# The last branch products and their merge in halves (block 1), and the dilated branch one unit earlier (block 2)

## What is computed

```
y = gates[:, :, 0] * (branches[0] @ w_branch[0])
for n in range(1, N_BRANCH):                       # N_BRANCH = 4
    y = y + gates[:, :, n] * (branches[n] @ w_branch[n])
return y @ w_out
```

```
merged = g_a * (y_a @ br_nsa) + g_b * (y_b @ br_dil) + g_c * (y_c @ br_fox)
return merged @ w_out
```

## Time and profile before

| | |
|---|---|
| time, median of 3 runs | 2589.56 us (2586.72 to 2591.66) |
| profiled execution | 2586.87 us, of which span 2585.1 us |
| granted TensorE clock, mean | 0.982 |
| PE busy | 2467.6 us (95%) |
| DVE busy | 1642.1 us (64%) |
| ACT busy | 1202.5 us (47%) |
| POOL busy | 214.4 us (8%) |

### The profile page before, as it was taken

One profiled execution on the slowest core, in us unless ns is written; L12 is line 12 of the kernel. 1 busy time (PEld: TensorE's weight loads), 2 busy tenths in 40 slices (PEclk: granted clock), 3 DMA queues, 4 the chain that ended last, 5 costly groups with the idle time before them and its releaser, 6 DMA issues.

```text
span 2585.1 us, 34304 instructions
## 1 busy us (share of the span) xinstructions
PE 2467.6 (95%) x14089; PEld 2107.8 (82%) x14089; DVE 1642.1 (64%) x2149; ACT 1202.5 (47%) x1441; POOL 214.4 (8%) x334
## 2 busy tenths in 40 slices
PE   7999998999999999899999999989999999998998
PEld 5888997788788899788778888877877879897786
DVE  4775777676776686767677565565455456556544
ACT  4435464433433546344443346934444443693443
POOL 2000002000100000300010000210000000021000
PEclk9999999999999999899999999999999999999999
DMA  8784455786786454678588554445646545444553
GB/s 288 258 287 152 148 168 181 253 290 232 262 285 227 141 151 161 203 261 283 192 276 297 199 149 138 131 157 191 207 154 215 185 157 158 136 134 163 196 185 107
DMA packets 369163, 514.27 MB, mean 199 GB/s; under 512 B 21600, under 2 KB 310614, under 8 KB 369008
## 3 DMA queue, kind: packets, MB, share of 16 engines
q1 hardware_dynamic: 342608, 415.80, 49.8%
q0 software_dynamic: 26400, 96.28, 10.5%
HBM read 510.89 MB, written 1.13 MB: 198 GB/s over the span
## 4 chain that ended last, share of the span: by engine, by line
PE 86%; DVE 6%; ACT 3%; issue 3%; DMA 0%; POOL 0%; SPq 0%; DVEq 0%; POOLq 0%; ACTq 0%
PE ps L1647 79%; DVE lo L1081 2%; PE ps L1693 2%; ACT hi L708 2%; PE ps L1795 1%; PE ps L1669 1%; PE ps L1823 1%; PE ps L1833 1%; PE ps L1842 1%; DVE arena L1140 1%; DMA raw<-in_ffn_w_gu 0%; DVE X L1114 0%; POOL arena L482 0%; DVE arena L1104 0%; ACT arena L748 0%
## 5 line engine op out<-in xcount | busy, mean ns | idle before, releaser
L1081 DVE TENSOR_TENSOR lo<-raw,hi 128x2048 fp32r<-128x2048 f32 (+1 forms) x400 | 916.4, 2292 | 593.1 <-ACT hi L708 592.3
L708 ACT ACTIVATE hi<-raw 128x2048 fp32r<-128x2048 f32 (+1 forms) x400 | 758.0, 1897 | 559.6 <-PE ps L1647 543.6
L1647 PE MATMUL ps<-hi,NH 128*128 128x512 f32 (+3 forms) x1760 | 683.6, 388 | 53.0 <-DVE NL L1569 28.1
L1647 PE MATMUL ps<-hi,NL 128*128 128x512 f32 (+3 forms) x1760 | 674.0, 383 | 0.0
L1647 PE MATMUL ps<-lo,NH 128*128 128x512 f32 (+3 forms) x1760 | 673.5, 383 | 0.0
L1647 PEld LDWEIGHTS ps<-hi,NH 128*128 128x128 f32 x1760 | 338.4, 192 | 127.2 <-DVE lo L1081 30.6
L1647 PE MATMUL ps<-NH,hi 128*128 128x256 f32 x1376 | 394.2, 286 | 0.0
L1647 PEld LDWEIGHTS ps<-hi,NL 128*128 128x128 f32 x1760 | 337.2, 192 | 67.6
L1647 PEld LDWEIGHTS ps<-lo,NH 128*128 128x128 f32 x1760 | 338.0, 192 | 65.0
L1647 PE MATMUL ps<-NL,hi 128*128 128x256 f32 x1376 | 388.0, 282 | 0.0
L1647 PE MATMUL ps<-NH,lo 128*128 128x256 f32 x1376 | 386.7, 281 | 0.0
(11 more groups left out here) (297 smaller groups left out, 2038.4 us busy)
## 6 DMA issues: line engine op xcount, KB each, us to landing
raw<-in_ffn_w_gu SPq DMA_DIRECT2D x176, 512.0 KB, 4.9
raw<-in_ffn_w_in SPq DMA_DIRECT2D x176, 512.0 KB, 4.7
arena<-in_ada_w POOLq DMA_DIRECT2D x72, 1024.0 KB, 7.1
raw<-in_w_in SPq DMA_DIRECT2D x96, 512.0 KB, 4.5
raw<-in_ffn_w_down SPq DMA_DIRECT2D x88, 512.0 KB, 4.7
raw<-in_ffn_w_out SPq DMA_DIRECT2D x88, 512.0 KB, 4.1
raw<-in_mix_w_in SPq DMA_DIRECT2D x86, 512.0 KB, 4.6
raw<-in_w_branch SPq DMA_DIRECT2D x16, 512.0 KB, 3.7
```

The source lines that it names most:

```text
L708: last = nc.scalar.activation(dst, src, ACT.Copy)
L1081: last = nc.vector.tensor_tensor(dst, src, part.bitcast(F32), ALU.subtract)
L1647: last = nc.tensor.matmul(dst, a, b, start=start and k == 0, stop=stop and k == 2, skip_group_check=skip)
```

## The change

Block 1: branches 2 and 3 are no longer multiplied one after the other. When units 27 and 28 are both there, TensorE takes pairs 0 and 1 of branch 2, pairs 0 and 1 of branch 3, then pairs 2 and 3 of branch 2 and of branch 3. Block 2: the dilated branch (n = 2) moves from unit 28 to unit 27, and the fox branch (n = 1) ends the stage alone: unit 27 holds its first chunk beside the dilated weight, unit 28 its other two. In both blocks VectorE and ScalarE merge pairs 0 and 1 ahead of the splits of unit 30, and pairs 2 and 3 behind them. VectorE's `yl` of a half stand after both `y` of that half.

```diff
                     elif u == BR2 + 1:
-                        pieces = rows(i["br_w_fox_2"][l], 0)
+                        pieces = [(lambda s: raw[:, s, 0:1024], i["br_w_fox_2"][l, 0:128, :]),
+                                  (lambda s: raw[:, s, 1024:2048], i["br_w_dil_2"][l])]
                     elif u == BR2 + 2:
-                        pieces = [(lambda s: raw[:, s, 0:1024], i["br_w_fox_2"][l, 256:384, :]),
-                                  (lambda s: raw[:, s, 1024:2048], i["br_w_dil_2"][l])]
+                        pieces = rows(i["br_w_fox_2"][l], 1)
...
-                    if s.block == 2 and u == BR2 + 2:
+                    if s.block == 2 and u == BR2 + 1:
                         for b in range(4):
                             pair = slice(2 * b, 2 * b + 2)
-                            pool.wait_ge(dve_done, at("dve", "gated 1" if b == 3 else f"gated 1 {b}"))
-                            nc.gpsimd.tensor_tensor(T8[:, pair, :], G2[:, pair, :], G2[:, 16 + 2 * b:18 + 2 * b, :],
+                            pool.wait_ge(dve_done, at("dve", "gated 2" if b == 3 else f"gated 2 {b}"))
+                            nc.gpsimd.tensor_tensor(T8[:, pair, :], G2[:, pair, :], G2[:, 8 + 2 * b:10 + 2 * b, :],
...
                     if u:
+                        if u == OUT1 - 1:
+                            gated_parts(range(0, 2))
                         split_hi(s, u + 2)
...
-                gated_parts()
+                gated_parts(range(2, 4))
...
+            def merged(gates, n, sum_before, pairs):
+
+                for b in pairs:
+                    gated(gates, n, (b,))
+                    mine(f"gated {n}" if b == 3 else f"gated {n} {b}")
+                    dve.wait_ge(pool_done, at("pool", f"{sum_before} {b}"))
+                    y = T8[:, 2 * b:2 * b + 2, :]
+                    nc.vector.tensor_tensor(y, y, gates[:, 2 * b:2 * b + 2, :], ALU.add).then_inc(dve_done, done("dve", f"y {b}"))
+                for b in pairs:
                     dve.wait_ge(act_done, at("act", f"yh {b}"))
                     nc.vector.tensor_tensor(NL[:, 2 * b:2 * b + 2, :], T8[:, 2 * b:2 * b + 2, :], NH[:, 2 * b:2 * b + 2, :].bitcast(F32),
                                             ALU.subtract).then_inc(dve_done, done("dve", f"yl {b}"))
...
                 for u in range(OUT1):
-                    if s.block == 2 and u == BR2 + 2:
-                        gated(G2[:, 16:24, :], 1, False, None)
+                    if u == OUT1 - 1:
+                        if s.block == 1:
+                            gated(G[:, 16:24, :], 2, range(0, 2))
+                            merged(G[:, 24:32, :], 3, "sum 2", range(0, 2))
+                            gated(G[:, 16:24, :], 2, range(2, 4))
+                        else:
+                            merged(G2[:, 16:24, :], 1, "sum 1", range(0, 2))
                     if u:
                         split_lo(s, u + 2)
...
+                    if u == OUT1 - 1:
+                        if s.block == 1:
+                            merged(G[:, 24:32, :], 3, "sum 2", range(2, 4))
+                        else:
+                            merged(G2[:, 16:24, :], 1, "sum 1", range(2, 4))
...
+                    if k < 2:
+                        branch_unit(s, k, [(0, 2 * k), (1024, 2 * k + 1)], True, True).then_inc(unit_used, 1)
+                    elif k == 3:
+
+                        ahead = (u - 1) % RING
+                        branch_unit(ahead, 2, [(0, 4), (1024, 5)], True, True, range(0, 2))
+                        branch_unit(s, 3, [(0, 6), (1024, 7)], True, True, range(0, 2))
+                        branch_unit(ahead, 2, [(0, 4), (1024, 5)], True, True, range(2, 4)).then_inc(unit_used, 1)
+                        branch_unit(s, 3, [(0, 6), (1024, 7)], True, True, range(2, 4)).then_inc(unit_used, 1)
...
                 elif u == BR2 + 1:
 
                     pe.wait_ge(act_done, at("act", f"ev {BR2 - 1}"))
-                    last = branch_unit(s, 1, [(0, 3), (1024, 4)], True, False)
+                    branch_unit(s, 1, [(0, 3)], True, False)
+                    last = branch_unit(s, 2, [(1024, 2)], True, True)
                 else:
-                    branch_unit(s, 1, [(0, 5)], False, True)
-                    last = branch_unit(s, 2, [(1024, 2)], True, True)
+                    last = branch_unit(s, 1, [(0, 4), (1024, 5)], False, True)
...
                 out_part(o, 0)
-                if s.block == 2:
+                if s.block == 1:
                     pe.wait_ge(dve_done, at("dve", "gated 2 2"))
                 out_part(o, 1).then_inc(unit_used, 1)
```

More of the change, by code:

```diff
@@ L642, in mix @@
                                                     ALU.add).then_inc(pool_done, done("pool", f"sum {k} {b}"))
-                    if s.block == 2 and u == BR2 + 2:
+                    if s.block == 2 and u == BR2 + 1:
                         for b in range(4):
                             pair = slice(2 * b, 2 * b + 2)
-                            pool.wait_ge(dve_done, at("dve", "gated 1" if b == 3 else f"gated 1 {b}"))
-                            nc.gpsimd.tensor_tensor(T8[:, pair, :], G2[:, pair, :], G2[:, 16 + 2 * b:18 + 2 * b, :],
+                            pool.wait_ge(dve_done, at("dve", "gated 2" if b == 3 else f"gated 2 {b}"))
+                            nc.gpsimd.tensor_tensor(T8[:, pair, :], G2[:, pair, :], G2[:, 8 + 2 * b:10 + 2 * b, :],
                                                     ALU.add).then_inc(pool_done, done("pool", f"sum 1 {b}"))
-                    if u == BR1 + (1 if s.block == 1 else 3):
+                    if u == BR1 + (1 if s.block == 1 else 2):
                         pool.wait_ge(pool_done, at("pool", "sum 1 3"))
@@ L1014, in exps, with gated_parts @@
                             nc.scalar.activation(DE[:, 0, :], DE[:, 0, :], ACT.Exp).then_inc(act_done, done("act", "dexp"))
-            def gated_parts():
-                for b in range(4):
+            def gated_parts(pairs):
+                for b in pairs:
                     act.wait_ge(dve_done, at("dve", f"y {b}"))
@@ L1563, in factors, with gated @@
                                 .then_inc(dve_done, done("dve", f"factor {n}"))
-            def gated(gates, n, last, sum_before):
-                def rest(b):
+            def gated(gates, n, pairs=range(4)):
+                for b in pairs:
+                    dve.wait_ge(pe_done, at("pe", f"br {n} {b}"))
+                    v = gates[:, 2 * b:2 * b + 2, :].rearrange("p a t -> p (a t)")
+                    nc.vector.tensor_tensor(v, v, ps[:, 4 * (1 - n % 2) + b, :], ALU.mult).then_inc(dve_done, done("dve", f"gated {n}" if b == 3 else f"gated {n} {b}"))
+            def merged(gates, n, sum_before, pairs):
+                for b in pairs:
+                    gated(gates, n, (b,))
[3 more added lines that the diff above has]
+                    nc.vector.tensor_tensor(y, y, gates[:, 2 * b:2 * b + 2, :], ALU.add).then_inc(dve_done, done("dve", f"y {b}"))
+                for b in pairs:
                     dve.wait_ge(act_done, at("act", f"yh {b}"))
@@ L1570, in rest @@
                                             ALU.subtract).then_inc(dve_done, done("dve", f"yl {b}"))
[L1572 to L1584, removed]
             def mix(s):
@@ L1607, in mix @@
                             side2(s, work)
-                    if s.block == 1 and u >= BR1:
+                    if s.block == 1 and u in (BR1, BR1 + 1):
                         k = u - BR1
-                        gated(G[:, 8 * k:8 * k + 8, :], k, k == 3, "sum 2")
+                        gated(G[:, 8 * k:8 * k + 8, :], k)
                     if s.block == 2 and u == BR2:
-                        gated(G2[:, 0:8, :], 0, False, None)
-                    if s.block == 2 and u == BR2 + 2:
-                        gated(G2[:, 8:16, :], 2, True, "sum 1")
+                        gated(G2[:, 0:8, :], 0)
+                    if s.block == 2 and u == BR2 + 1:
+                        gated(G2[:, 8:16, :], 2)
+                    if u == OUT1 - 1:
[3 more added lines that the diff above has]
+                            merged(G2[:, 16:24, :], 1, "sum 1", range(2, 4))
                 split_lo(s, OUT1 + 2)
@@ L1866, in unit1, with branch_unit @@
                         pe.wait_ge(act_done, at("act", f"ev {BR1 - 1}"))
-                    branch_unit(s, u - BR1, [(0, 2 * (u - BR1)), (1024, 2 * (u - BR1) + 1)], True, True).then_inc(unit_used, 1)
+                    k = u - BR1
+                    if k < 2:
[6 more added lines that the diff above has]
+                        branch_unit(s, 3, [(0, 6), (1024, 7)], True, True, range(2, 4)).then_inc(unit_used, 1)
                     return
                 last.then_inc(unit_used, 1)
-            def branch_unit(s, n, chunks, first, final):
+            def branch_unit(s, n, chunks, first, final, pairs=range(4)):
                 base = 4 * (1 - n % 2)
-                for k in range(C):
```

(1 more changed line is left out.)

## The result

The changed kernel takes 2563.99 us (median of 4 runs, 2560.75 to 2569.46) against 2588.2 us; the ratio is 0.9906, with an interval of 0.9895 to 0.9918, so 24 us faster. Forecast were 13.4 us and a range of 2567 to 2583. The waits that the change shortens were the right ones; two terms of the sum were too small, and the time lies under the range.

The account below looks back on a forecast made before the run. PE, busy 95%, plus its waits bounds the kernel; only waits could pay, 28.1 us for `NL`. Block gains 2 x 2.4 + 2 x 4.3 = 13.4 us take 2589.56 to 2576.2; 2575.5 us was named, range 2567 to 2583.

Parts of the forecast that it names:

- the demand to have both units of weights: Block 1, start of the alternating halves: costs nothing unless VectorE were over 1 us later.
- the next stage's loads: Behind the boundary: first unit's load comes 4 us later but stays covered; without that cover it would cost 4 us.
- The three waits per boundary: PE before (29,0), (30,0), (31,0): 1.6, 4.0, 0.5 us in block 1; 1.0, 2.2, 0.6 us in block 2.
- Rivals 1 and 2: At boundaries: merge only moves the wait, 2585 us (chance 0.10); more or longer clock falls, slower, 2593 us (0.06).
- rival 3: Block 1: lo 30 gets in after one add; 0.7 us less a stage, 1.4 in all, 2574 us; chance 0.20.
- The waits saved: Four boundaries, without any clock effect: 2 x 1.8 + 2 x 2.4 = 8.4 us, called the firm part.
- As in the earlier trace I let it wait for both adds: Block 1: lo 30 begins at 419.0, waits for both GpSimd adds to 420.8, ends 2.2 us later at 423.0.
- The clock: Boundaries: half-clock time after waits, up to 2.0 us each; a fall remains in block 1, none in block 2.
- 2 x 2.4: Block 1's two boundaries: gain of 2.4 us each with a clock fall, 3.8 us if the clock stays up.
- rival 4: No clock falls at the boundaries: 16.2 us, perhaps 4 more from another stretch, 2569 to 2573 us; chance 0.12.
- the start of the sum: Whole kernel before: median of the runs, 2589.56 us, which would become 2576.2.

Follow-up runs that it names:

- e6: Kernel before with GpSimd's `sum 2` of block 1 left out, so branch 2 is missing from the output: 2578.22 us, ratio 0.9961.
- e11: The changed kernel, unaltered, run once more for a second profile and more runs: 2565.45 us, ratio 0.9922.
- e7: Kernel before with GpSimd's load of the gain row moved behind `sum 2` in block 1: 2581.86 us, ratio 0.9972.
- e10: Kernel before with the gain row's load behind `sum 2` in block 1 and a tiny GpSimd operation in its old place: 2581.87 us, ratio 0.9976.
- e5: Kernel before with 96 (block 1) or 64 (block 2) small matmuls of zeros in TensorE's wait at the four boundaries: 2580.48 us, ratio 0.9970.
- e12: Changed kernel with weight quarters ordered 0, 2, 1, 3, gain row loaded behind the sums, 48 zero matmuls in each mixing stage's norm wait: 2556.01 us, ratio 0.9881.
- e15: Changed kernel with output weight quarters ordered 0, 2, 1, 3 and gain row loaded behind the sums, without zero matmuls: 2557.78 us, ratio 0.9877.
- e16: As e15, run beside it, plus 48 zero matmuls in the norm's wait of each of the four mixing stages: 2557.85 us, ratio 0.9878.

## Why the prediction was right in kind and wrong in size

Right: that only PE's waits for `NL` could pay; that the lo of unit 30 behind GpSimd's adds was what made `yl 1` late (e6); that `y 0` would wait for `sum 2 0` and `sum 2 1`, and that the demand to have both units of weights costs nothing; that lo 28, the next stage's loads and the gain row would hide. The three waits per boundary came in the order forecast. Rivals 1 and 2 did not happen; rival 3 (the lo gets in after one add) was the true course of the adds.

Wrong were two terms: 13.4 us were forecast, 22.5 measured, and of the 9 us between them the waits are some 6 and the clock some 3.

1. *The waits saved*: I had 8.4 us, measured are 15.4 for `NL` less 0.6 to 0.9 more for `lo`, some 14.5. In block 1 the forecast 1.6 + 4.0 + 0.5 = 6.1 measures 1.33 + 2.73 + 0.29 = 4.4 (e11), in block 2 1.0 + 2.2 + 0.6 = 3.8 measures 0.64 + 1.64 + 0.29 = 2.6. The one step that was wrong in kind is "As in the earlier trace rows I let it wait for both adds": it waited for one. That alone gave some 0.6 of the 1.7 us in block 1, since the lo took 3.00 instead of 4.0 but `y 2` 1.08 instead of 0.69, much as rival 3 has it (0.7). I had taken the odd one of four cases in the rows (two lo and a `y` got in after one add, the lo of 412.31 after four) for the rule. By the Trainium skill's page "SBUF — State Buffer", section "Who interferes with whom", the lock is held for one instruction; e7, e10 and the profile after agree with it, and the 6.56 us of the earlier trace rows do not. The rest, 1.1 us a stage in block 1 and 1.2 in block 2, is small amounts at the hand-overs, nearly all added on the same side. In block 2, for example, `yl 1` was there 0.35 us earlier than worked out, and the two (29,·) parts end 0.24 us later than 24 x 0.232 says (1708.14 - 1.63 - 1700.70 = 5.81).
2. *The clock*: I had 5.0 us, by one fall in each boundary of block 1 after, none in block 2, and none gained elsewhere. The runs give some 8 (22.5 less 14.5), known to 3 us either way. At the boundaries the falls cost 7.8 us before (e5). After, block 2 has none, as I took it; in block 1 e11 has a fall at the second boundary alone and the first profile at both, each some 1.5 us, so 5 to 6.5 us are saved there. The step "2 x 2.4" was thus right for the runs with both falls and too low for the others. What is left, up to 3 us, would lie outside the boundaries, where I had no term: behind like waits elsewhere, such as the earlier trace rows, the clock fell in some profiles of either kernel and not in others. Whether the changed kernel really has fewer such falls stays open.

The mean clocks say little for it. They count a low clock in a wait too, where it costs nothing. The first boundary before, and the second in e11, the one that has a fall (columns as in the earlier trace rows):

```profile
418.00:430.00 12.00, 5.80 (x17) 0.57 0.41 127
```

```profile
1052.00:1058.00 6.00, 5.48 (x17) 0.72 0.62 178
```

The first stretch lacks 0.43 of its 12 us, 5.2 us of full clock, the second 1.7. The four boundaries before lack 17 us in this way, those after 1.7 (e11) to 3.4 (first profile), so they alone lift the mean by 14 to 15 us of full clock. The step from 0.982 to 0.988 is 15 to 16.

The range failed with the two terms. It held rival 3 and rival 4 one at a time; what happened was rival 3, small errors nearly all of one sign, and about the clock gain of rival 4 (7.8 us), together 14.5 + 8. The mean of the nine runs, 2565.7 us, lies 1.3 us under the range too, and about as much comes from the start of the sum, 2589.56 us for the kernel before where more runs give 2588.2.

## What to carry to other kernels

A wait is best traced to the instruction that fills it: here one subtraction three times its usual length, behind adds of GpSimd whose sums were needed only later. Before an interleaving of matmuls is written, look which engine the merge really waits for; the halves of VectorE's queue did the work here and TensorE's alternation did none. And where TensorE stands still for some microseconds, count the half-clock stretch behind it as part of the wait: of the 22.5 us of this change some 8 were clock. Where a forecast adds up many hand-overs, each a little too long, that excess is a term of its own: it was 4 to 5 us here.

## What was not expected of the hardware

- A load issued by GpSimd 0.6 us ahead of four adds let all four go before VectorE's subtraction (6.56 us); with a tiny operation in its place the subtraction got in after one (2.50 us, e10). Moving one load was worth 6 to 7 us of the kernel (e10, e7).
- Matmuls of zeros in a wait made the kernel 7.8 us faster (e5), but 48 of them at four other waits, where they also kept the clock at 1.00 (e12), nothing that could be told (e15, e16).
- The same instructions with the same wait of 2.7 us were followed by a clock fall in one profile and not in another, and the nine runs of the changed kernel spread over 11 us with their mean clock, the five of e11 by 2.4 us for each 0.001.
